# Gate and up weights laid with eight neighbouring rows in a partition, and token rows transposed from every eighth column

## The reference, cut to what matters

```python
N_EXPERTS = 16; TOP_K = 2; D_EXPERT = 256          # w_gate, w_up: (DEPTH, 16, 1024, 256); w_down: (DEPTH, 16, 256, 1024)
def grouped_moe(h, w_router, b_router, w_gate, w_up, w_down):
    ...                                             # best group of four experts, then the best two in it: gate_dense
    hg = jnp.einsum('td,edf->tef', h2, w_gate)
    hu = jnp.einsum('td,edf->tef', h2, w_up)
    act = jax.nn.silu(hg) * hu * gate_dense[:, :, None].astype(h2.dtype)
    y = jnp.einsum('tef,efd->td', act, w_down)
```

## Time and profile before

| | us |
|---|---|
| median of three runs | 953.28 |
| the runs, lowest and highest | 950.37 and 957.61 |
| the profiled execution | 953.39 |
| its span | 951.6 |

### The profile page before, as it was taken

One profiled execution on the slowest core, in us unless ns is written; L12 is line 12 of the kernel. 1 busy time (PEld: TensorE's weight loads), 2 busy tenths in 40 slices (PEclk: granted clock), 3 DMA queues, 4 the chain that ended last, 5 costly groups with the idle time before them and its releaser, 6 DMA issues.

```text
span 951.6 us, 12318 instructions
## 1 busy us (share of the span) xinstructions
PE 892.7 (94%) x4438; PEld 624.3 (66%) x4438; DVE 539.7 (57%) x1098; ACT 376.7 (40%) x755; POOL 125.6 (13%) x137
## 2 busy tenths in 40 slices
PE   6999999997999999989999999999999999998982
PEld 4887777874656656437878886877885565665531
DVE  4444886557666776474342224665366777666437
ACT  3322886001555556231132225776201455555300
POOL 2000332112010000041000001223011201000031
PEclk9999999998999999999999999999999999999997
DMA  9942000119999999572053223110117999999362
GB/s 323 350 157 85 13 1 1 45 65 320 343 361 347 365 357 373 208 263 91 0 198 113 89 89 112 45 46 26 64 45 283 315 350 363 349 352 371 121 211 88
DMA packets 106853, 183.14 MB, mean 192 GB/s; under 512 B 6496, under 2 KB 72032, under 8 KB 106800
## 3 DMA queue, kind: packets, MB, share of 16 engines
q1 hardware_dynamic: 92864, 132.34, 40.9%
q0 software_dynamic: 9200, 33.33, 10.8%
q10 hardware_dynamic: 4736, 16.78, 4.6%
HBM read 159.60 MB, written 22.84 MB: 192 GB/s over the span
## 4 chain that ended last, share of the span: by engine, by line
PE 87%; DVE 5%; DMA 3%; issue 2%; POOL 1%; ACT 1%; POOLq 0%; SPq 0%; DVEq 0%; ACTq 0%
PE bank L519 17%; PE bank L520 17%; PE bank L521 17%; PE bank L764 12%; PE bank L648 5%; PE bank L614 4%; PE bank L631 3%; PE bank L733 2%; PE bank L474 2%; PE bank L500 2%; PE bank L488 1%; DMA arena<-ys,pos 1%; PE bank L683 1%; PE bank L656 1%; DMA ring<-in_swa_w_in 1%
## 5 line engine op out<-in xcount | busy, mean ns | idle before, releaser
L1272 DVE TENSOR_TENSOR low<-ring,gu_high 128x1024 fp32r<-128x1024 f32 x128 | 151.2, 1221 | 55.8 <-ACT gu_high L960 55.8
L960 ACT CAST gu_high<-ring 128x1024 fp32r<-128x1024 f32 x128 | 127.7, 1048 | 21.4 <-DVE arena L1407 16.1
L764 PE MATMUL bank<-ring,arena 128*96 128x512 f32 x256 | 118.3, 606 | 7.3 <-issue 5.0
L519 PE MATMUL bank<-gu_high,rows_high 128*96 128x512 f32 x256 | 113.4, 443 | 2.5 <-DVE rows_low L1391 2.5
L520 PE MATMUL bank<-low,rows_high 128*96 128x512 f32 x256 | 101.9, 398 | 0.0
L521 PE MATMUL bank<-gu_high,rows_low 128*96 128x512 f32 x256 | 101.3, 396 | 0.0
L764 PEld LDWEIGHTS bank<-ring,arena 128*96 128x96 f32 x256 | 39.6, 164 | 62.9 <-issue 62.8
L908 ACT ACTIVATE arena<-arena,nmax 128x256 f32<-128x256 f32 (+3 forms) x128 | 66.8, 522 | 30.9 <-DVE nmax L1203 20.2
L519 PE MATMUL bank<-high,x_high 128*128 128x512 f32 x160 | 65.3, 408 | 6.8 <-DVE low L1099 5.3
L422 POOL TENSOR_TENSOR low<-ring,high 128x512 fp32r<-128x512 f32 x32 | 40.6, 1270 | 231.9 <-ACT high L928 231.9
L648 PE MATMUL bank<-arena 128*128 128x64 f32 x544 | 68.1, 269 | 0.2 <-ACT arena L922 0.2
(11 more groups left out here) (207 smaller groups left out, 1475.7 us busy)
## 6 DMA issues: line engine op xcount, KB each, us to landing
ring<-in_w_gate SPq DMA_DIRECT2D x32, 1024.0 KB
ring<-in_w_up SPq DMA_DIRECT2D x32, 1024.0 KB
ring<-in_w_down SPq DMA_DIRECT2D x32, 1024.0 KB, 14.6
ys<-arena ACTq DMA_DIRECT2D x32, 384.0 KB
ring<-in_fox_w_in SPq DMA_DIRECT2D x6, 2048.0 KB
ring<-in_swa_w_in SPq DMA_DIRECT2D x3, 2048.0 KB
ring<-in_swa_w_o SPq DMA_DIRECT2D x2, 2048.0 KB
xd<-xres ACTq DMA_DIRECT2D x8, 512.0 KB, 2.7
```

The lines of the kernel that those rows point to most:

```text
L519: eng.matmul(out, ah, wh, start=(c == 0), stop=False)
L764: mm = eng.matmul(bank[5 + half][0:CAP, :], hT[:, b, c, :], w[:, c, half * BLK:(half + 1) * BLK], start=(c == 0), stop=(c == FC - 1))
L960: eng.copy(gu_high[u % 2][:, part, :], slot_in(use)[:, part, :]).then_inc(S("gu_high"), 1)
L1272: eng.tensor_tensor(lows[use % RING][:, part, :], slot_in(use)[:, part, :], gu_high[u % 2][:, part, :], ALU.subtract).then_inc(S("gu_low"), 1)
```

## The change

The gate and up loads take eight neighbouring rows of the weight matrix into a partition: chunk c of partition p is now row 8p + c, which is `(p c)` instead of `(c p)`. A partition's part of a gate load is then one piece of 8 KB. In the slot gate lies as a whole ahead of up (`[P, 2, KC, F]`) where chunk by chunk 256 words of gate stood beside 256 of up. So the moving operand of each of the 24 matmuls is now two runs of 256 words, 8 KB apart, where it was one run of 512; each part of the split is two runs of 512 words where it was one of 1024. To match, `turn_rows` takes every eighth column of the token rows, from column c on: 128 words that lie 32 bytes apart, where 128 neighbouring words stood. The number of instructions on every engine and their order stay as they were, and so do the down weights, the attention's weights and the semaphores. `lows` stays for the attention's weights, `gu_low` names the same bytes for the experts.

```diff
-        gu_high = [nc.alloc_sbuf_tensor_at("gu_high0", [P, KC, BLK], fp32r, offset=arena_at + 4 * 11648),
-                   nc.alloc_sbuf_tensor_at("gu_high1", [P, KC, BLK], fp32r, offset=xT_at)]
+        gu_high = [nc.alloc_sbuf_tensor_at("gu_high0", [P, 2, KC, F], fp32r, offset=arena_at + 4 * 11648),
+                   nc.alloc_sbuf_tensor_at("gu_high1", [P, 2, KC, F], fp32r, offset=xT_at)]
...
+        gu_low = [nc.alloc_sbuf_tensor_at(f"gu_low{i}", [P, 2, KC, F], fp32r, offset=ring_at + 4 * i * SLOT_WORDS) for i in range(RING)]
...
+        def slot_gate_up(k):
+            return ring[:, k % RING, 0:KC * BLK].rearrange("p (g c f) -> p g c f", g=2, c=KC)
...
-                gu = slot_in(s)
-                eng.dma_start(gu[:, :, 0:F], w_gate[w, e].rearrange("(c p) f -> p c f", p=P)).then_inc(sem, 16)
-                eng.dma_start(gu[:, :, F:2 * F], w_up[w, e].rearrange("(c p) f -> p c f", p=P)).then_inc(sem, 16)
+                gu = slot_gate_up(s)
+                eng.dma_start(gu[:, 0, :, :], w_gate[w, e].rearrange("(p c) f -> p c f", p=P)).then_inc(sem, 16)
+                eng.dma_start(gu[:, 1, :, :], w_up[w, e].rearrange("(p c) f -> p c f", p=P)).then_inc(sem, 16)
...
                 def turn_rows(b):
+                    rows = xe[0:CAP, b, :].rearrange("p (d c) -> p c d", c=KC)
                     for c in range(KC):
-                        mm = eng.transpose(bank[c // 4][:, (c % 4) * P:(c % 4) * P + CAP], xe[0:CAP, b, c * P:(c + 1) * P], ident[0:CAP, 0:CAP])
+                        mm = eng.transpose(bank[c // 4][:, (c % 4) * P:(c % 4) * P + CAP], rows[:, c, :], ident[0:CAP, 0:CAP])
...
                         mm = three(bank[2 + b][0:CAP, :], rows_high[:, b, c, :], rows_low[:, b, c, :],
-                                   gu_high[b][:, c, :], lows[use % RING][:, c, :], c)
+                                   gu_high[b][:, :, c, :], gu_low[use % RING][:, :, c, :], c)
...
-                        eng.copy(gu_high[u % 2][:, part, :], slot_in(use)[:, part, :]).then_inc(S("gu_high"), 1)
+                        eng.copy(gu_high[u % 2][:, :, part, :], slot_gate_up(use)[:, :, part, :]).then_inc(S("gu_high"), 1)
...
-                        eng.tensor_tensor(lows[use % RING][:, part, :], slot_in(use)[:, part, :],
-                                          gu_high[u % 2][:, part, :], ALU.subtract).then_inc(S("gu_low"), 1)
+                        eng.tensor_tensor(gu_low[use % RING][:, :, part, :], slot_gate_up(use)[:, :, part, :],
+                                          gu_high[u % 2][:, :, part, :], ALU.subtract).then_inc(S("gu_low"), 1)
```

More of the change, by code:

```diff
@@ L745, in gate_up_split @@
                         mm = three(bank[2 + b][0:CAP, :], rows_high[:, b, c, :], rows_low[:, b, c, :],
-                                   gu_high[b][:, c, :], lows[use % RING][:, c, :], c)
+                                   gu_high[b][:, :, c, :], gu_low[use % RING][:, :, c, :], c)
                     return mm
                 def gate_up(b, use):
-                    w = slot_in(use)
+                    w = slot_gate_up(use)
                     for c in range(KC):
-                        mm = eng.matmul(bank[2 + b][0:CAP, :], xeT[:, b, c, :], w[:, c, :], start=(c == 0), stop=(c == KC - 1))
+                        mm = eng.matmul(bank[2 + b][0:CAP, :], xeT[:, b, c, :], w[:, :, c, :], start=(c == 0), stop=(c == KC - 1))
                     return mm
```

## The result

The changed kernel takes **946.45 us** (median of 7 runs, 946.01 to 948.71) against 953.28, a ratio of 0.9933 with a 95% interval of 0.9913 to 0.9952. It is faster by 0.7%, where 983 us had been forecast. The profiled execution took 946.05 us, its span is 944.3. One run of the kernel before, in a later comparison, took 1281.17 us at a granted clock of 0.65 and is left out of all ratios.

The account below looks back on a forecast made before the run. TensorE, never idle in an expert's 10.1 us period, was taken as the bound. 953.4 - 4.2 (larger pieces) + 34.0 (stride) = 983 us; own range 968 to 991, for 8 in 10 945 to 991.

Parts of the forecast that it names:

- The stride, +34.0 us: Token transposes on TensorE: loading every eighth column costs 133 ns more each, times 256 transposes, +34.0 us.
- the limit on which both engines agree: One 16-byte piece per 1.7 to 1.8 ns on VectorE and TensorE, giving 215 ns per strided transpose.
- the lowest price that I took from VectorE: Strided transposes: 0.64 ns a word more, times 128, gives 164 ns per transpose; +21.0 us in total.
- rival 1: Stride costs TensorE nothing or under 35 ns a transpose; only the DMA gain is left, 949 us; chance 0.30.
- Nothing covers it: The slower token transposes show in full, since down waits behind `turn_rows` in TensorE's own order.
- nothing is idle in that period: TensorE's 10.1 us expert period has no idle time, so a longer TensorE instruction is paid 32 times.
- Larger pieces, -4.2 us: Gate and up loads at 410 instead of 357 GB/s remove the second layer's stall: -4.2 us, between 0 and -4.2.
- late down load: Read as cause of the gap at the second layer's eleventh expert, which costs 2.5 + 1.7 = 4.2 us.
- The first gather, 0: TensorE's wait for the first layer's first gather and its clock fall: taken as 0, at best -4.5 us.
- rival 2: Stride cheap as in rival 1, and the first layer's gather early enough to keep the clock: 945 us; chance 0.05.
- Two runs in the moving operand, 0: One break more in the moving operand of 768 split matmuls costs 0, at most 1.4 us.
- rival 3: Thin transposes make TensorE's clock fall among the experts, about 1060 us; chance 0.08 of over 992, dearer stride included.

Follow-up runs that it names:

- the doubled version: Eight token transposes of each expert done twice: in the changed kernel 972.44 us, in the kernel before 967.3 us.
- the pair with the copy moved ahead: Changed kernel with VectorE's copy of the hidden rows ahead of two of three subtractions, 945.29 us; the same with the stride undone, 943.83 us.
- The filler experiment: Kernel before with 36 instead of 26 filler matmuls ahead of the first layer's first transposes: 954.49 us, ratio 1.0005.
- the version with the copy ahead: Kernel before with VectorE's copy of the hidden rows put ahead of two of the three subtractions: 947.38 us, ratio 0.994.
- the two filler versions: Kernel before with 36 instead of 26 fillers ahead of the first transposes, 954.49 us; changed kernel with 8 instead of 13 ahead of rank matmuls, 948.3 us.

## Why the prediction was wrong

**The stride, +34.0 us: the step that failed.** It failed twice. *The size:* I took VectorE's price for a word that lies alone and TensorE's own streaming of moving rows, "the limit on which both engines agree", and put it on a load of the stationary operand. Measured are 28 to 29 ns a transpose, in the spacing and in the doubled version, not 133. Even the lowest price that I took from VectorE (82 ns more) was almost three times too dear, and the value below 35 ns that rival 1 named was the true one. In the open it would have been 256 x 29 = 7.4 us. (The 42 ns between lines 1322 and 1325 are 0.66 ns a word and not 0.64, which would have moved the term by half a microsecond.) *The cover:* "Nothing covers it" and "nothing is idle in that period" were read from PE rows alone. The PEld rows show idle time ahead of most down products, up to 0.47 us and 0.18 on average in layer 1, where they wait for VectorE's copy of the hidden rows. With it only 1.9 us are left among the experts. That the gap is what hides it is shown expert by expert by the distances (0.66 becomes 0.89, 0.90 stays), by the doubled transposes (28 ns each once it is used up) and by the pair with the copy moved ahead (1.9 becomes 3.5). The page "Advanced Engine Details and Errata" of the Trainium skill, section SBUF Cachelines, has two accesses to one 16-byte line cost less than lone ones: every second column would be cheaper than every eighth. The runs show 216 ns and 203, against 142 without a stride. For this operand the measurement decides against it.

**Larger pieces, -4.2 us: right in size, wrong in its cause.** -4.3 us were measured, in one profile each, in layer 2 as said. But it was no late down load. From the kernel before, ScalarE and VectorE ahead of the stall in the earlier trace rows:

```profile
853.99 2.94 ACT L960 CAST gu_high<-ring 128x1024 fp32r<-128x1024 f32 x3 [3.39 <-DMA ring<-in_w_up]
855.07 3.50 DVE L1272 TENSOR_TENSOR low<-ring,gu_high 128x1024 fp32r<-128x1024 f32 x3 [4.36 <-ACT gu_high L960]
...
858.48 0.35 DVE L1397 COPY arena<-bank 128x192 f32<-128x192 f32 x1
...
858.90 0.24 PEld L764 LDWEIGHTS bank<-ring,arena 128*96 128x96 f32 x2 [2.67 <-issue]
```

The *up* load of the next expert is late, ScalarE's cast waits for it, VectorE's three subtractions wait for the cast, and the copy of the hidden rows, whose operands had been ready since TensorE's two transposes, stands behind them in VectorE's queue. The down product's first load starts 0.07 us after that copy ends, as in ordinary experts, so it waited for nothing later; TensorE's row names only "issue". Moving the copy ahead didn't take the loss away: another late up load cost about as much in its profile. The 410 GB/s taken for large pieces alone were about right. In the changed kernel the first gate and up loads of layer 2 run alone, and while the queue is busy all the time they reach (columns as in the earlier trace rows)

```profile
554.00:555.00 1.00, 1.00 (x6) 0.82 (x5) 0.00 (x0) 0.00 (x0) 0.00 (x0) 1.00 0.99 418
555.00:556.00 1.00, 1.00 (x6) 0.82 (x5) 0.00 (x0) 0.00 (x0) 0.00 (x0) 1.00 1.07 451
556.00:557.00 1.00, 1.00 (x6) 0.77 (x6) 0.00 (x0) 0.29 (x1) 0.00 (x0) 1.00 0.97 410
```

where 1 KB pieces had 337 to 379. The page "DMA: Bandwidth & Descriptors" of the Trainium skill, section Specifications, wants 512 B for line rate; by it this term was to be 0, and the rates of 347 with 1 KB and 387 GB/s with 8 KB speak against that here.

**The first gather, 0: too little.** It was -3.0 us, inside the bounds given (at best -4.5). In the eight profiles with pieces of 4 KB or more TensorE doesn't wait for it; of the seven with 1 or 2 KB and the same filler it waits 1.75 to 2.37 us in five, 0.25 us in one and not at all in one. So rival 2 (945 us, a chance of 0.05) is the one that came about, a cheap stride and a first gather early enough to keep the clock, and of the 3.0 us some 2.2 are the clock's. Why the gather comes early with large pieces wasn't tested by itself. The filler experiment adds a caution: with small pieces the same 2.7 us were given back. I take it that the loads and not TensorE then set the time, and that the change keeps them only because its loads are faster as well; one profile of each is all that says so.

**Two runs in the moving operand, 0: right**, by the version with that alone (1.0004); split matmuls still come 0.23 us apart.

**The clock** (rival 3) didn't fall among the experts: granted 1.00 from 742 to 909 us.

**The sum of what happened**, on the span: -4.3 + 1.9 - 3.0 = -5.4 us, and -1.9 in stretches that vary as much without a known cause; measured -7.3. The time lies inside the stated 945 to 991 us only because that range was drawn down to the rivals' figures. The forecast's own range, 968 to 991, doesn't hold it, and a time within 1% of before had a chance of 0.29.

## What to carry to other kernels

Before an instruction on the busiest engine is priced as fully exposed, look at the rows of its weight loads next to it: a matrix engine that looks full by its matmuls can have a gap in most periods, and a longer instruction ahead of a gap is free up to its width. Read that width in every period, not in one: here it went from 0 to 0.47 us. Follow a stall marked "issue" through the queues of the engines that feed it; a late load can reach an instruction that doesn't use it, and the place of that instruction in its queue is worth a trial of its own. Look then at where in the span the gain lies: the version with the copy ahead was as fast as the changed kernel, yet most of its profile's gain lay where the edit does nothing. And where loads run close to the period, a gain elsewhere may be given back until the loads have slack.

## What the runs showed of the hardware

- A float32 load of the stationary operand, 96x128, takes 142 ns from neighbouring words, 216 from every second and every fourth, 203 from every eighth; the transposes then come 111 ns apart instead of 82 (every eighth), and eight of them cost 0.23 us where nothing covers them. The step matters less than that there is one.
- An up load of 1 MB in 1024 pieces of 1 KB holds SP for 0.58 to 7.13 us in the kernel before, 0.58 where no load was under way (553.97 us); in pieces of 8 KB for 0.43 to 0.57 us.
- Gate and up loads alone ran at 337 to 379 GB/s in 1 KB pieces (556 to 561 us of the kernel before) and at 410 to 451 in 8 KB pieces (554 to 557 us of the changed kernel); beside other traffic, in the same 12 us, at 347 with 1 KB, 363 with 2, 386 with 4 and 387 with 8.
- A load from neighbouring addresses that lands in 1 KB pieces is as slow as one from scattered addresses (351 against 347 GB/s in the same window).
- In the comparison with the two filler versions the runs of the kernel before spread over 948.7 to 958.3 us (22 runs), those of the changed kernel over 946.9 to 947.8 (6 runs). I take the spread to be stalls that differ from run to run, since the profiles of kernels with 1 KB pieces show none to three of them among the experts; single runs without a profile can't show it.
